# First block of a two-part network on one core: the order of the projections of its recurrent branch changed, and VectorE's wide passes placed between their token shifts

## The reference

```python
p_rwkv, p_q, p_k, p_v, p_gate = _split_last(h @ w_in[l], (RWKV_COLS, ...))
# RWKV_COLS = 3 * 1024 (r, k, v) + 64 + 64 + 160 (low-rank inputs wd, ad, gd)

p = token_shift(p.astype(jnp.float32), mu)      # p + (previous token - p) * mu
r, k, v, wd, ad, gd = _split_last(p, ...)
w = -jax.nn.softplus(-(w0 + jnp.tanh(wd) @ w2)) - 0.5
decay = jnp.exp(-jnp.exp(w))
a = jax.nn.sigmoid(a0 + ad @ a2)
g = jax.nn.sigmoid(gd) @ g2
kk = heads(k * k_k)
kk = kk / jnp.maximum(jnp.sqrt(jnp.sum(kk * kk, axis=-1, keepdims=True)), 1e-12)
k = k * (1.0 + (a - 1.0) * k_a)
wkv = wkv7_scan(rh, heads(decay), kh, vh, -kk, kk * ah)      # a recurrence over the tokens
...
bonus = jnp.sum(rh * kh * r_k, axis=-1, keepdims=True) * vh
return (y + bonus.reshape(B, S, RWKV_WIDTH)) * g
```

## Time and profile before

| | us |
|---|---|
| median of three executions | 3342.66 (3341.81 to 3343.6) |
| the profiled execution, device time | 3343.02 |
| its span in the trace, first to last instruction | 3340.7 |
| TensorE busy | 3223.5 |
| VectorE busy | 1182.4 |
| ScalarE busy | 571.5 |
| mean granted TensorE clock | 0.984 of full speed |

### The profile page before, as it was taken

How to read it: one execution, slowest core, us unless ns; L and a number is a source line. 1 busy time by engine, 2 the same in 40 slices (tenths; PEclk the granted TensorE clock), 3 DMA queues, 4 the chain that set the end, 5 groups by cost and what they waited for, 6 DMA issues and landing times.

```text
span 3340.7 us, 41579 instructions
## 1 busy us (share of the span) xinstructions
PE 3223.5 (96%) x17876; PEld 2688.6 (80%) x17876; DVE 1182.4 (35%) x2020; ACT 571.5 (17%) x1127; POOL 0.2 (0%) x4
## 2 busy tenths in 40 slices
PE   8999889999999999999999999999999999899998
PEld 7888668788888875888568887888888788678887
DVE  1002543342012436534773345434424514621101
ACT  1001422131002111210440112111021210411100
POOL 0000000000000000000000000000000000000000
PEclk9999999999999999999999999999999999999999
DMA  5344443324434210232013132221232232133332
GB/s 202 139 154 151 156 151 126 126 76 191 152 136 153 84 68 32 95 129 93 31 51 139 76 152 101 76 101 53 97 116 76 73 135 79 68 139 126 136 141 101
DMA packets 29610, 374.27 MB, mean 112 GB/s; under 512 B 3072, under 2 KB 5248, under 8 KB 5504
## 3 DMA queue, kind: packets, MB, share of 16 engines
q1 hardware_dynamic: 29296, 370.75, 29.9%
q10 hardware_dynamic: 144, 1.05, 0.1%
HBM read 370.74 MB, written 1.05 MB: 111 GB/s over the span
## 4 chain that ended last, share of the span: by engine, by line
PE 90%; DVE 6%; ACT 2%; issue 1%; DMA 0%; SPq 0%; DVEq 0%; ACTq 0%
PE bank L754 90%; DVE small L2982 1%; PE bank L757 1%; ACT arena L2140 0%; DVE arena L2701 0%; DVE arena L2511 0%; DVE h_T L2300 0%; ACT h_T L1755 0%; ACT arena L2151 0%; DMA masks<-first_consts_dram 0%; DVE arena L2525 0%; DVE arena L2992 0%; DVE factors L2403 0%; DVE h_T L2283 0%; ACT arena L1787 0%
## 5 line engine op out<-in xcount | busy, mean ns | idle before, releaser
L754 PE MATMUL bank<-h_T,weights 128*128 128x256 f32 (+1 forms) x5296 | 1240.3, 391 | 25.7 <-ACT masks L1787 5.9
L754 PEld LDWEIGHTS bank<-h_T,weights 128*128 128x128 f32 x5296 | 1007.5, 192 | 223.4 <-issue 81.6
L754 PE MATMUL bank<-arena,weights 128*128 128x256 f32 x2840 | 628.8, 382 | 5.7 <-DVE arena L2779 2.5
L754 PEld LDWEIGHTS bank<-arena,weights 128*128 128x128 f32 x2840 | 542.2, 191 | 86.4 <-issue 5.7
L754 PE MATMUL bank<-factors,weights 128*128 128x256 f32 x1432 | 323.7, 379 | 1.9 <-DVE factors L2403 1.3
L754 PEld LDWEIGHTS bank<-factors,weights 128*128 128x128 f32 x1432 | 271.8, 190 | 39.6 <-issue 1.7
L2420 DVE TENSOR_TENSOR arena<-bank,arena 128x512 f32<-128x512 f32 (+1 forms) x132 | 88.1, 667 | 430.0 <-PE bank L754 428.5
L1803 ACT ACTIVATE arena<-bank 128x512 f32<-128x512 f32 (+1 forms) x144 | 83.3, 579 | 696.2 <-PE bank L754 661.5
L754 PE MATMUL bank<-arena 64*64 64x64 f32 (+7 forms) x1592 | 184.5, 305 | 13.6 <-ACT arena L2151 9.0
L2334 DVE TENSOR_TENSOR arena<-arena,bank 128x256 f32 (+1 forms) x66 | 27.8, 422 | 426.3 <-PE bank L754 426.3
L754 PEld LDWEIGHTS bank<-arena 64*64 64x64 f32 (+2 forms) x1592 | 128.8, 160 | 58.2 <-ACT arena L2151 24.1
(11 more groups left out here) (300 smaller groups left out, 2284.8 us busy)
## 6 DMA issues: line engine op xcount, KB each, us to landing
weights<-wide_slabs_dram SPq DMA_DIRECT2D x151, 2048.0 KB, 7.7
weights<-down_slabs_dram SPq DMA_DIRECT2D x32, 1408.0 KB, 5.8
masks<-second_consts_dram SPq DMA_DIRECT2D x1, 2240.0 KB, 8.7
masks<-second_consts_dram SPq DMA_DIRECT2D x2, 1024.0 KB, 7.1
x_T<-x_T_dram SPq DMA_DIRECT2D x1, 1024.0 KB, 5.8
x_T<-ctx_T_dram SPq DMA_DIRECT2D x1, 1024.0 KB, 11.3
out_dram<-h_T ACTq DMA_DIRECT2D x1, 1024.0 KB, 3.9
masks<-first_consts_dram SPq DMA_DIRECT2D x1, 928.0 KB, 7.4
```

The costliest lines, as they stand in the source:

```text
L754: return mm(out, lhsT, rhs, start=start, stop=stop, skip_group_check=True)
```

## The change

The stages come in another order: low-rank input, k, low-rank output, r (two halves), v (two halves), with a modulation slab behind the first half of each, then both gate halves, then the other ten modulation slabs. The modulation slabs and the halves of r and v are now stages of their own. On VectorE the passes that need no receptances and values are put between the shifts of the tiles of r and v, one to a tile; the reciprocal is cut into four and the scans into two groups of four. ScalarE squares `k * k_k` within the low-rank output, takes the roots ahead of r, and makes the exponentials behind tiles 5, 6 and 7 of r. The bonus product is kept in another buffer (`X2`, since the shift buffer is still in use), and V is brought to token order last instead of first. The diff, cut:

```diff
 (stage_list)
-    for n in ("r", "k", "v"):
-        add("rwkv_" + n, 2, 4, 4, 0)
     add("rwkv_lora_in", 1, 3, 3, 0)
-    add("rwkv_gate0", 1, 4, 4, 0)
+    add("rwkv_k", 2, 4, 4, 0)
     add("rwkv_lora_out", 1, 24, 24, 0)
-    add("rwkv_gate1", 1, 4, 4, 0)
-    add("ada0", 12, 1, 0, 0)
+    for n, name in enumerate(("r0", "r1", "v0", "v1")):
+        add("rwkv_" + name, 1, 4, 4, 0)
+        if n % 2 == 0:
+            add(f"ada0_{n // 2}", 1, 1, 0, 0)
+    gates("rwkv")
+    for n in range(2, 12):
+        add(f"ada0_{n}", 1, 1, 0, 0)
 (TensorE)
+            project(ST["rwkv_lora_in"], lambda k: H1[:, k], T, drains=by_act, part=(0, 3), ready=1)
+            project(ST["rwkv_k"], lambda k: H1[:, k], T, drains=by_act, frees=act_frees("rwkv_lora_in", 3) + act_frees("rwkv_lora_in", 1))
             st = ST["rwkv_lora_out"]
             arrived(st, 0)
             t.wait("lora_ready")
...
+            head_sums("act_for_pe", slot3(sKH), "pe_for_act")
+            pe.wait_ge(S["cond_ready"], 1)
+            for name, before in (("r0", "lora_out"), ("r1", "r0"), ("v0", "r1"), ("v1", "v0")):
+                project(ST["rwkv_" + name], lambda k: H1[:, k], T, drains=by_act, frees=act_frees("rwkv_" + before))
+                ada_fill()
+            gate("rwkv", 0, act_frees("rwkv_v1"))
+            pe.wait_ge(S["ada_free"], 3)
+            head_sums("dve_for_pe", X2[:, :, T:2 * T], "pe_for_dve")
+            gate("rwkv", 1, act_frees("rwkv_gate0"))
...
+            enter(ST["ada0_2"])
+            inputs(3)
+            to_tokens("Bt", 0, sBH)
+            ada_fill()
+            to_tokens("Kt", 4, sKH)
+            ada_fill()
+            ada_fill()
+            to_tokens("Vt", 8, sV)
+            for _ in range(2):
                 ada_fill()
 (ScalarE)
+            for q in range(3):
+                shift_in("lora_in", q)
+            shift_in("k", 0)
+            act.wait_ge(S["shift_done"], 3)
...
+            for q in range(1, 8):
+                shift_in("k", q)
             for q in range(24):
+                if q == 9:
+                    t.wait("dve_for_act")
+                    t.out(af(slot(sKH), slot(sA), ACT.Square), "act_for_pe")
...
+            for q in range(8):
+                shift_in("r", q)
+                if q == 3:
+                    ada_fill()
+                elif q == 5:
+                    t.wait("dve_for_act")
+                    t.out(af(slot(sBH), slot(sL), ACT.Exp), "act_for_dve")
+                elif q == 6:
+                    t.out(af(slot(sKH), slot(sL), ACT.Exp, scale=-1.0), "act_for_dve")
+                elif q == 7:
+                    t.out(af(slot(sL), G[:, HALF:2 * HALF], ACT.Exp), "act_for_dve")
+                    ada_fill()
 (VectorE)
+            for q in range(8):
+                shifted("r", q)
+                if q == 0:
+                    t.wait("act_for_dve")
+                    say("ada_free")
+                    t.step(ts(L, L, -math.exp(-0.5), None, mul))
+                    t.step(nc.vector.tensor_copy(lm, L))
+                elif q == 1:
+                    decay_scan(range(4))
+                elif q == 2:
+                    decay_scan(range(4, KT))
+                elif q == 3:
+                    t.out(tt(lm, L, lm, sub), "dve_for_act")
+                elif q == 4:
+                    t.step(ts(slot(sB), slot(sB), 1e-12, None, ALU.max))
+                else:
+                    part_reciprocal(q - 5)
+            for q in range(8):
+                shifted("v", q)
+                if q == 1:
+                    for _ in range(2):
+                        ada_fill()
+                if q == 0:
+                    part_reciprocal(3)
+                elif q == 1:
+                    t.step(tt(slot(sA), slot(sA), slot(sB), mul))
+                elif q == 2:
+                    t.step(tt(slot(sB), slot(sA), slot(sAA), mul))
+                elif q == 3:
+                    t.step(ts(slot(sAA), slot(sAA), -1.0, None, add))
+                elif q == 4:
+                    t.step(tt(slot3(sAA), slot3(sAA), bc(pc("k_a", 0, 8), 2, T), mul))
+                elif q == 5:
+                    t.step(stt(slot(sK), slot(sAA), 1.0, slot(sK), add, mul))
+                elif q == 6:
+                    t.step(tt(rk, R3, K3, mul))
+                else:
+                    t.out(tt(rk, rk, bc(pc("r_k", 0, 8), 2, T), mul), "dve_for_pe")
```

More of the change, by code:

```diff
@@ L381, in both @@
                 job(name, c)
-    for name in ("Vt", "Bt", "Kt"):
+    for name in ("Bt", "Kt", "Vt"):
         for c in range(NCH):
@@ L1053, in _, with head_sums @@
                     last.then_inc(S["tile_done"], 1)
-            gate("rwkv", 1, act_frees("rwkv_lora_out"))
-            ada_st = ST["ada0"]
+            def head_sums(ready, src, done):
+                t.wait(ready)
+                for b in range(4):
+                    last = matmul(bank[4 + b][:, :], pair, src[:, 2 * b:2 * b + 2])
+                last.then_inc(S[done], 1)
+            head_sums("act_for_pe", slot3(sKH), "pe_for_act")
             ada_step = [0]
@@ L1856, in _, with ada_fill, shift_in @@
             t.wait("dve_for_act")
[L1857 to L1867, removed]
+            ada_step = [0]
+            def ada_fill():
+                j, half = divmod(ada_step[0], 2)
+                ada_step[0] += 1
+                if half == 0:
+                    ada_row_out(ST[f"ada0_{j}"], 0)
+            n_shift = [0]
+            def shift_in(name, q):
+                st, first = shift_stage(name, q)
+                n = n_shift[0]
+                n_shift[0] += 1
+                act.wait_ge(S["tile_done"], st.done0 + q - first + 1)
+                if n >= 4:
+                    act.wait_ge(S["shift_done"], n - 3)
+                af(shift[:, n % 4, 1:257], bank[q % 4][:, 0:T], ACT.Copy).then_inc(S["act_out"], 1)
+            for q in range(3):
+                shift_in("lora_in", q)
+            shift_in("k", 0)
+            act.wait_ge(S["shift_done"], 3)
             lora = tiles(A, sBH * HALF, 4, T)
@@ L2493, in _ @@
             t.out(nc.vector.memset(shift[:, :, 0:1], 0.0), "dve_for_act")
-            n = 0
             dif = H[:, HALF + 1040:HALF + 1296]
-            for name, base in (("r", sR), ("k", sK), ("v", sV), ("lora_in", sBH)):
-                st = ST["rwkv_" + name]
-                for q in range(st.slabs * st.act):
-                    dve.wait_ge(S["act_out"], st.act0 + q + 1)
-                    cur, prev = shift[:, n % 4, 1:257], shift[:, n % 4, 0:256]
-                    rows = slice(0, P) if n < 26 else slice(0, 32)
-                    t.step(tt(dif[rows], prev[rows], cur[rows], sub))
-                    t.out(stt(slot3(base)[rows, q], dif[rows], pc("mu", n)[rows], cur[rows], mul, add), "shift_done")
-                    n += 1
@@ new lines, in by_chunk @@
+            def by_chunk(k):
+                return slot(k).rearrange("p (k c t) -> p k c t", k=KT, t=CHUNK)
+            dcol = bc(dec, 3, CHUNK)
+            for _ in range(2):
+                ada_fill()
+            t.wait("act_for_dve", 2)
+            t.step(nc.vector.tensor_copy(dec, by_chunk(sBH)[:, :, :, CHUNK - 1]))
+            t.step(tt(slot(sB), slot(sB), slot(sKH), mul))
+            t.step(tt(slot(sR), slot(sR), slot(sBH), mul))
+            t.out(tt(by_chunk(sBH), by_chunk(sB), dcol, mul), "wkv_inputs")
@@ L2541, in _ @@
+            t.step(tt(slot(sK), slot(sK), slot(sKH), mul))
+            t.out(tt(by_chunk(sKH), by_chunk(sK), dcol, mul), "wkv_inputs")
+            t.wait("act_for_dve")
+            t.step(stt(slot(sA), slot(sA), -1.0, slot(sL), mul, mul))
             t.wait("pe_for_dve")
```

161 lines of the change are left out of this document (55 added, 106 removed).

## The result

The changed kernel took 3314.51 us in the median of four executions (3312.72 to 3319.95) beside 3343.13 for the kernel before (3341.81 to 3346.09): a ratio of 0.9913, 95% interval 0.99 to 0.9925, thus 28.6 us or 0.86% faster. The forecast was 3316.2, with a range of 3311.5 to 3321.5. The profiled execution took 3312.72 us, its span 3310.9.

A forecast was written before the change was run, and what follows sets the result against it. TensorE, busy 96% of the span, was taken as the bound. First transposition 20.9 us earlier plus 5.5 at the transpositions made 26.4 us off 3343.02: 3316.6, less 0.36 for the median, 3316.2 us; range 3311.5 to 3321.5.

The forecast's parts named there:

- The sum: First transposition at 406.9 instead of 427.80, 20.9 us, plus 5.5 at the transpositions: 26.4 us, carried to the end.
- Part 1: Low-rank input, then keys: low-rank output starts without a wait, 2.2 us on L1889 go; nothing taken for it.
- Part 2: Square of the keys inside the low-rank output: new TensorE stall of 1.0 us, bounds 0 and 3.2.
- Part 3: Receptances and values over VectorE's passes: 11 us of slack at two places; waits of 8.3, 3.2 and 1.6 us go.
- the rival of an edit that does nothing: The hole is caused by something other than VectorE's chain, so 3342 us would stand; chance 0.01.
- Part 4: At the first transposition TensorE waits for ScalarE's drain of the last gate tile: 0.7 us, bounds 0.5 and 1.5.
- Part 5: Transpositions spread among modulation steps, up to the grams: 20.3 us instead of 25.83, winning 5.5 us.
- Part 6: Weight slabs in a ring of three land in time, tightest with 9 us to spare; priced at nothing.
- The clock: Rival: the clock falls again in the low-rank stretch or transpositions, 1.2 to 1.7 us each, 3319; chance 0.12.
- VectorE became the bound: Rival: VectorE's passes grow by 40% beside the projections, leaving 11 us on the path, 3327 us; chance 0.04.
- A starved ring: Rival: weight slabs land late and stop TensorE at every half, 3350 us, slower than before; chance 0.01.
- the list of losses: TensorE's waits and slow-clock losses before the grams, 25.4 us, less 1.0, 0.7 and 0.6: 23.1 us as the least gain.

The follow-up runs named there:

- the repeat: Kernel after, unchanged, measured once more: 3321.24 us in the median, ratio 0.9935 to the kernel before.
- the smoothed one: Kernel after with the keys' square cut into four pieces between low-rank drains and a modulation row product ahead of the first transposition: 3314.64 us, ratio 0.9919.
- the two kernels with late passes: Kernel after with the first bonus-product pass made four or eight times more on VectorE: 3314.22 and 3323.07 us, one execution each.
- the old token order: Kernel after with V, B, K brought to token order in that order and three, one, one modulation steps: 3320.28 us, ratio 0.9939.
- its filler: Kernel before with 18 useless matmuls on TensorE between the first and second modulation pair, where it waits 7.7 us: 3336.85 us, ratio 0.9984.

## Why the forecast was right, and where it was not

**The sum** stands. The transposition was forecast at 406.9 and came at 406.91, the grams at 427 and came at 426.87. The gain of the region was to be 26.4 us and is 26.9. That the two places agree to 0.1 and 0.3 us is in part luck: the first tiles took 0.6 us longer in this trace than in the two others of the same kernel (41.06 us for eleven tiles, 40.50 and 40.47 there), and the grams come 171.5 to 171.8 us after the first projection in those. What the whole run shows beyond it is scatter of the code after it, which had a term of 2 to 3 us in the range; the traces since show 9 us between the extremes, so that term was too small. The median of the repeat, 3321.24, lies just inside the range.

**Part 1, the start of the low-rank output,** was right: it starts at 295.84 without a wait, and the 2.2 us on L1889 are gone.

**Part 2, the square,** was right: the idle time shown is 0.62 us, in the place that was stepped to, but from start to start the low-rank output takes 14.70 us in the kernel after (310.54 - 295.84) and 13.82 in the smoothed one, so the stall costs 0.9 us of the 1.0 forecast. It is ScalarE's queue, as the smoothed kernel shows: with the same square in pieces the stall is gone.

**Part 3** was right in its numbers and wrong in its reason. VectorE's load between the shifts, its lag and its slack came out as worked out (10.8 us against 11), a wait of 27.69 without the passes between the shifts against 26 to 27, and the two kernels with late passes bear out the slack on either side. But the text named the reciprocal as the longest piece of the chain, put the hole down to VectorE, and held against the rival of an edit that does nothing that the chain goes through VectorE without a break. The expectation of the experiment without the reciprocal went by the same reading, with 14 us for the reciprocal alone, where 0.9 came. The step that failed is the reading of the chain itself: it names what ended a wait last, and the decay's scaling waited for two things. The low-rank output's last drain came at 386.5, and the reciprocal's product ended at 387.4. What would be late next was not asked there. In the sum this did no harm, since the change moves the low-rank output too and the sum was built up from TensorE's own work instead of taken off the chain. The rival that the text lacked is the one of a half change, and it would have been priced at nothing.

**Part 4, the wait at the first transposition,** is 0.56 us against 0.7 (0.6 from start to start: 14.54 us for the gate half, where 13.9 are its own).

**Part 5** was to win 5.5 us and won 5.9 (25.83 to 19.96). The text counted 2.2 us of waits for the row copy towards it, but of their three places only one, 0.72 us, lies behind 427.80; the other two are in the hole. The spread of the steps is a small share of the gain, 0.6 to 1.6, as the old token order shows. The sum wasn't hurt, since it was added up from the pieces.

**Part 6** was right: no wait of TensorE names a weight load in the whole region.

**The rivals.** The clock did not fall again within the region: the 30 records after the gap of 0.62 us inside the low-rank output took 6.58 us, the full-speed pitch. The Trainium skill ("TensorE: Matmul & The Clock Gate", section "A second HAM failure mode: psum-queue depth-cycling") tells of a kernel in which frequent short idles between groups of matmuls make the clock swing between its two levels. In this region nothing of that kind is seen, with idles of 0.3 to 0.6 us. In the kernel before with its filler, waits of 1.48, 1.02 and 0.33 us one after another were followed by a head sum of 5.40 us, between the 3.60 and 6.77 of the two levels, which agrees with it; that these waits were the cause is not shown, since the head sum took 5.40 us without the filler too, in the kernel with the reciprocal twice. VectorE became the bound only with eight passes more. A starved ring was not seen.

## What to carry to other kernels

A chain of waits names one releaser for each step; before a gain is taken off it, read in the code what else that step waits for and when it came, because two paths of one length give nothing when only one is shortened. Building the sum up from the bound engine's own work, piece by piece at its full-speed durations, gave the gain of the region within 1 us, where the list of losses gave 23.1 as the least and left almost 4 us open. And where a long chain on a second engine can be cut into passes of the size of the bound engine's pitch, the overruns of single turns don't matter as long as the buffers between them hold more than the lag: here a lag of up to 3 us and four places of 3.5 us each. No run shows what a smaller buffer would cost.

## What the runs showed of the hardware

The granted clock fell in some executions and not in others at the same instruction: in the kernel after, the first column product behind the grams took 1.05 us in one trace and 1.86 in another. The low-rank stretch of the kernel before took 13.44 us in its trace, and in the trace with the filler, which comes 18 us behind that stretch, 11.76, after the same wait of 2.20 us. Over a whole run such dips moved the span by 9 us with the instructions unchanged, where the executions of the kernel before had shown less than 2 us when the forecast was made (3341.81 to 3343.6; beside the experiments it took 3335.47 to 3352.07).

A reciprocal over 128x512 takes 3.35 us and one over 128x2048 12.95, so cutting it into four cost 0.45 us in all.
